# Running sums of softplus values as products of split fp32r halves, with the next head's scores issued earlier, in a two-layer hybrid encoder on one Trainium2 core

## The chip, the cores and the metric

The kernel runs on one core of a Trainium2 chip. Its time is the device time of one execution in microseconds. Three runs of the kernel before took 3045.1, 3046.19 and 3046.79 us; the median, 3046.19 us, is the number to compare with.

The engines are named as in the profile: PE is TensorE's matmul side and PEld its weight loads, DVE is VectorE, ACT is ScalarE, POOL is GpSimd, SP is SyncE, whose queue issues the weight transfers.

## The reference

The input is 512 tokens of 1024 features. Each of two layers runs a half-step SwiGLU FFN, a mixer, a second half-step FFN and a gated embedding. The mixer projects its input and runs three token mixers beside each other: RWKV-7, stick-breaking attention and HGRN2. The change is in the attention, with four heads of 128 features. For query q and key k let z = q·k / sqrt(128). In the reference:

```
m      = where(k < q, -softplus(z), 0)
within = sum of m over the keys of the same block of 128 from k onwards
carry  = sum of m over all later blocks of keys
att    = where(k < q, exp(z + within + carry), 0)
y      = att @ v
```

So the logit of a key is its score, less the softplus values of this key and of all later keys up to the query. That running sum along the keys is what the change computes in another way.

## The kernel before

**Dense products.** All large products run in fp32r. An fp32 value is split into a high fp32r part and the rest, and a product is three fp32r products (high by high, rest by high, high by rest), issued in `products` (L864 to L885, the matmul is L881). The weights arrive in slots of 256 rows by 512 columns through a ring of three raw buffers: SP's queue loads them (L1254), POOL splits each slot in four instructions (L1226 high part, L1229 rest, for two halves) into a ring of three split buffers. POOL waits for a split buffer until PE has used the slot that was in it three slots ago (L1217), and SP waits for POOL (L1250).

**Filling.** `dense` (L893) is a generator: each step issues one block, three fp32r products of 512 columns. PE's program runs small, latency-bound work of the mixers and calls `advance(fill, n)` (L990) to put n blocks of dense work between its parts. During the attention the filling is `hg_projections` (L1054): four groups of projections, n = 0 to 3, each with four result tiles and 32 blocks, in PSUM banks 0 to 3. Blocks 29 to 32 of a group complete its four tiles.

**Attention, per head h, on PE** (L1086 to L1108). PSUM banks 4 to 7 are for it (`core_banks`).

- Scores: for each block of 128 keys kb = 3, 2, 1, 0, one fp32 product of the queries from kb on (128, 256, 384, 512 columns) into a bank of its own (L1090).
- 16 blocks of filling.
- Sums: for kb = 3 to 0 it waits for the softplus values of block kb (`sb_sp`, L1094). Then, for each k2 from kb to 3, it adds one fp32 product onto the scores: constants (a triangle of -1 for k2 = kb, all -1 for k2 > kb) times the softplus values of block k2 (L1096). These are 10 products in a head, with 2560 columns together. In the trace each fp32 product is two records.
- 8 blocks of filling, the product of `att` with the values (L1103), 8 blocks of filling.

**On ACT** (L1568 to L1609), in this order for a head: absolute values of the scores (L1574), exp (L1578), ln(1 + ...) (L1582), each for the four kb; in head 2 a logarithm for the HGRN2 gate (L1449), in head 3 the absolute values, two exponentials and a logarithm for it; the exponential of the logits (L1595), which waits for the sums; the copy of y out of PSUM (L1603); `hgrn_inputs(L, h)` (L1398 to L1415, L1607), which waits for the four tiles of filling group n = h, one after the other, and evacuates them; after head 1, an absolute value and an exponential of 2048 columns (L1442, L1443). Then come the absolute values of head h + 1.

**On DVE** (L1924 to L1946): for kb = 3 to 0 the softplus value max(z, 0) + ln(...) with z read from PSUM (L1932) and the causal mask on its diagonal block (L1935), whose end is the signal `sb_sp` for PE. From head 1 on, a wait for the last sums of the previous head stands before it (L1931). Later the mask on the exponentials (L1943), whose end is the signal `sb_att`. In head 2 the operations of `forget_gate` follow (L1874), in head 3 those of `forget_rate` (L1885) stand before L1943.

Of the kernel before, what the change touches and what calls it, by code (L numbers as in the profile page):

```python
# [21 lines left out]
F32 = mybir.dt.float32  # L22
# [6 lines left out]
P = 128  # L29
D = 1024  # L30
SEQ = 512
# [106 lines left out]
def build(nc, a, out, counts, banks_of):  # L138
# [4 lines left out]
    with ctx:  # L143
# [57 lines left out]
        with ExitStack() as own:  # L201
            y_raw = sb(own, "y_raw", [P, 3, 4, SEQ])
            sb_sp, sb_att = y_raw[:, 1, :, :], y_raw[:, 2, :, :]
            o3 = ExitStack()
            rw_u = sb(o3, "rw_u", [P, 3, SEQ + 1])
            rw_d = sb(o3, "rw_d", [P, SEQ])
            lora_x = sb(o3, "lora_x", [P, 3, SEQ])
            with ExitStack() as o1:
                hg_q = sb(o1, "hg_q", [P, 4, SEQ])
                hg_k = sb(o1, "hg_k", [P, 4, SEQ])  # L210
                hg_p = sb(o1, "hg_p", [P, 4, SEQ])
                hg_x = sb(o1, "hg_x", [P, 4, SEQ])
                hg_v = sb(o1, "hg_v", [P, NT, 512])
                hg_g = sb(o1, "hg_g", [P, NT, 512])
                hg_e = sb(o1, "hg_e", [P, 2, 1024])
                with ExitStack() as o2:
                    sb_q = sb(o2, "sb_q", [P, 4, SEQ])
                    sb_k = sb(o2, "sb_k", [P, 4, SEQ])
                    sb_v = sb(o2, "sb_v", [P, NT, 512])
                    sb_e = sb(o2, "sb_e", [P, 4, SEQ])  # L220
                with ExitStack() as o2:
                    hg_Q = sb(o2, "hg_Q", [P, 4, SEQ])
                    hg_K = sb(o2, "hg_K", [P, 4, SEQ])
                    hg_att = sb(o2, "hg_att", [P, 2, NT, 4, HALF])
                    hg_S = sb(o2, "hg_S", [P, NT, 4, P])
            with ExitStack() as o2:


                rkv = sb(o2, "rkv", [P, 3, SEQ])
                starts = sb(o2, "starts", [P, SEQ])  # L230
                w_up = sb(o2, "w_up", [P, 512])
                g_up = sb(o2, "g_up", [P, 2, 512])
                rk_sum = sb(o2, "rk_sum", [P, 4, P])
                rw_sw = sb(o2, "rw_sw", [P, SEQ])
                rw_a = sb(o2, "rw_a", [P, SEQ])
                rw_cs = sb(o2, "rw_cs", [P, SEQ])
                rw_e3 = sb(o2, "rw_e3", [P, SEQ])
                rw_e1 = sb(o2, "rw_e1", [P, SEQ])
                rw_kk = sb(o2, "rw_kk", [P, SEQ])
                rw_ss = sb(o2, "rw_ss", [P, SEQ])  # L240
                bonus_v = [sb(o2, "bonus_v0", [P, SEQ])]
                rw_keep = sb(o2, "rw_keep", [P, SEQ])
                pq_add = sb(o2, "pq_add", [P, 2, NT, 2, HEAD])
                xl = sb(o2, "xl", [P, 2 * NT, HEAD])
                inv = sb(o2, "inv", [P, 2 * NT, HEAD])
                invT = sb(o2, "invT", [P, 2 * NT, HEAD])
                pq = sb(o2, "pq", [P, 2, NT, 2, HEAD])
                bm = sb(o2, "bm", [P, 2, NT, 2, HEAD])
                km = sb(o2, "km", [P, 2, NT, 2, HEAD])
                rw_dec = sb(o2, "rw_dec", [P, 2, SEQ])  # L250
                ar = sb(o2, "ar", [P, NT, 2, P])
                b_inv = sb(o2, "b_inv", [P, SEQ])
                k_inv = sb(o2, "k_inv", [P, SEQ])
                b_tok = sb(o2, "b_tok", [P, NT, P])
                k_tok = sb(o2, "k_tok", [P, NT, P])
                yt = sb(o2, "yt", [P, 2, NT, P])
                bonus_v.append(sb(o2, "bonus_v1", [P, SEQ]))
                rhs = sb(o2, "rhs", [P, 2, NT, P])
                xx = sb(o2, "xx", [P, 2, NT, P])
                v_tok = sb(o2, "v_tok", [P, 2, NT, P])  # L260
                gn_st = sb(o2, "gn_st", [P, 2, NT, 2])

            rw_bd, rw_kd = rw_dec[:, 0, :], rw_dec[:, 1, :]
            rw_b, rw_k2 = rw_ss, rw_sw
            d_mat = rhs[:, 0, :, :].rearrange("p t (c n) -> p (t c) n", c=2)
            s_all = rhs[:, 1, :, :].rearrange("p t (c n) -> p (t c) n", c=2)
            o3.close()
            with ExitStack() as o2:
                yT = [sb(o2, "yT_hi", [P, 4, SEQ], F32R), sb(o2, "yT_lo", [P, 4, SEQ], F32R)]
                gate_s = sb(o2, "gate_s", [P, 4, SEQ])  # L270
                m_tmp = sb(o2, "m_tmp", [P, SEQ])
                m_acc = sb(o2, "m_acc", [P, KD, SEQ])
                mT = [sb(o2, "mT_hi", [P, KD, SEQ], F32R), sb(o2, "mT_lo", [P, KD, SEQ], F32R)]
# [43 lines left out]
        def of_units(x, height, which):  # L317

            return x.rearrange("p u (n two s) -> p u n two s", two=2, s=height)[:, :, :, which, :]

        def of_parity(x, odd):

# [508 lines left out]
        def _(pe):  # L831
# [213 lines left out]
            for L in range(DEPTH):  # L1045
# [37 lines left out]
                for m in range(4):  # L1083
                    for n in range(3):
                        pe.wait_ge(*after("sb_in", L, n, m))
                for h in range(4):  # L1086
                    zb = {}
                    for kb in range(3, -1, -1):
                        zb[kb] = take(("sbz", L, h, kb), ("sb_exp", L, h, kb), core_banks)
                        nc.tensor.matmul(zb[kb][:, kb * P:SEQ], sb_k[:, h, kb * P:(kb + 1) * P], sb_q[:, h, kb * P:SEQ],  # L1090
                                         start=True, stop=False, skip_group_check=True).then_inc(*step("sbz_done", L, h, kb))
                    advance(fill, 16)
                    for kb in range(3, -1, -1):
                        pe.wait_ge(*after("sb_sp", L, h, kb))  # L1094
                        for k2 in range(kb, 4):
                            ins = nc.tensor.matmul(zb[kb][:, k2 * P:SEQ], cons[:, K_NTRI if k2 == kb else K_NONE, :],  # L1096
                                                   sb_sp[:, k2, k2 * P:SEQ], start=False, stop=k2 == 3, skip_group_check=True)
                        ins.then_inc(*step("sb_logit", L, h, kb))
                    advance(fill, 8)
                    o = take(("sby", L, h), ("sb_y", L, h), core_banks)  # L1100
                    for kb in range(4):
                        pe.wait_ge(*after("sb_att", L, h, kb))
                        ins = nc.tensor.matmul(o[:, kb * P:SEQ], sb_v[:, kb, h * P:(h + 1) * P], sb_att[:, kb, kb * P:SEQ],  # L1103
                                               start=kb == 0, stop=kb == 3, skip_group_check=True)
                    ins.then_inc(*step("sby_done", L, h))
                    if h == 3:
                        hgrn_pairs(-1)
                    advance(fill, 8)  # L1108
                run(fill)

                def all_projections():
# [628 lines left out]
        def _(dve):  # L1740
# [160 lines left out]
            for L in range(DEPTH):  # L1901
# [12 lines left out]
                else:  # L1914
# [5 lines left out]
                    chain(v.tensor_tensor(lb_log, lb_s, lb_rest, ALU.subtract))  # L1920
                    v.tensor_scalar(lb_rest, lb_rest, -1.0, None, ALU.mult).then_inc(*step("lb_set", L))
                now("lb_set", L)

                for h in range(4):  # L1924
                    for kb in range(3, -1, -1):
                        b = ps[banks_of.get(("sbz", L, h, kb), 0)]
                        cols = slice(kb * P, SEQ)
                        diag = slice(kb * P, kb * P + P)
                        now("sb_ln", L, h, kb)
                        if h:  # L1930
                            now("sb_logit", L, h - 1, 0)  # L1931
                        v.scalar_tensor_tensor(sb_sp[:, kb, cols], b[:, cols], 0.0, sb_e[:, kb, cols], ALU.max, ALU.add).then_inc(  # L1932
                            *step("sb_sp0", L, h, kb))
                        now("sb_sp0", L, h, kb)
                        v.tensor_tensor(sb_sp[:, kb, diag], sb_sp[:, kb, diag], cons[:, K_CAUSAL, :], ALU.mult).then_inc(  # L1935
                            *step("sb_sp", L, h, kb))
                    if h == 3:
                        forget_rate(L)
                    for kb in range(3, -1, -1):
                        diag = slice(kb * P, kb * P + P)  # L1940
                        now("sb_exp", L, h, kb)

                        v.scalar_tensor_tensor(sb_att[:, kb, diag], sb_att[:, kb, diag], 3e38, cons[:, K_CAUSAL, :], ALU.min,  # L1943
                                               ALU.mult).then_inc(*step("sb_att", L, h, kb))
                    if h == 2:
                        forget_gate(L)  # L1946
# [185 lines left out]
```

## Time and profile before

| | us |
|---|---|
| median of three runs | 3046.19 |
| the profiled execution, its own time | 3044.86 |
| span of the profiled execution | 3043.1 |
| PE busy | 2947.1 |
| POOL busy | 2312.5 |
| DVE busy | 1362.2 |
| ACT busy | 652.6 |

The profile is that of one execution. Busy times overlap, so they don't add up to the span. Matmuls are pipelined: a record of 0.39 us is followed by the next 0.23 us later, so the spacing of the starts is what a matmul costs. Layer 0's attention lies at 451 to 569 us of the span, layer 1's at about 1963 to 2081.

### The profile page before, as it was taken

How to read it: one execution, taken by the hardware profiler on the slowest of the kernel's cores; microseconds unless marked ns; L12 is line 12 of the kernel's file. 1: busy time of each engine (PE TensorE's matmuls, PEld its weight loads, DVE VectorE, ACT ScalarE, POOL GpSimd, SP SyncE). 2: the span in 40 equal slices, each digit the busy share in tenths (PEclk: the TensorE clock that was granted, in tenths of full speed). 3: DMA queues.
4: the chain of work that ended last, by engine and by line, in shares of the span. 5: the costliest groups of instructions: out<-in, count | busy, mean ns of one | idle time of the engine just before them, and what ended most of it. 6: DMA issues, size and time to landing. Idle time of an engine off the chain costs nothing.

```text
span 3043.1 us, 48203 instructions
## 1 busy us (share of the span) xinstructions
PE 2947.1 (97%) x20354; PEld 2392.3 (79%) x20354; DVE 1362.2 (45%) x1833; ACT 652.6 (21%) x1069; POOL 2312.5 (76%) x1853
## 2 busy tenths in 40 slices
PE   8999999999899999999999999999998999999997
PEld 7888877776678888888788888777766788888886
DVE  4221133786647462220752212437766465622118
ACT  1000125554310020000420002246543100200003
POOL 8998896662259989888689887966521699899874
PEclk9999999999999999999999999999999999999999
DMA  4332242121113333333323332421210233333332
GB/s 137 104 97 98 90 132 71 48 59 38 30 57 97 125 97 104 98 96 97 104 88 100 100 96 89 133 69 48 56 42 23 70 94 128 97 104 97 97 97 97
DMA packets 202068, 266.65 MB, mean 88 GB/s; under 512 B 12369, under 2 KB 130493, under 8 KB 201853
## 3 DMA queue, kind: packets, MB, share of 16 engines
q1 hardware_dynamic: 194624, 243.51, 26.5%
q10 hardware_dynamic: 7228, 20.05, 1.8%
q8 instruction: 162, 2.65, 0.4%
q14 instruction: 54, 0.43, 0.0%
HBM read 257.22 MB, written 6.29 MB: 87 GB/s over the span
## 4 chain that ended last, share of the span: by engine, by line
PE 83%; DVE 7%; POOL 5%; issue 2%; ACT 2%; DMA 0%; SPq 0%; DVEq 0%; POOLq 0%; ACTq 0%
PE ps L881 73%; POOL w_hi L1226 3%; POOL w_lo L1229 3%; PE ps L449 1%; PE ps L1096 1%; PE ps L1074 1%; PE ps L928 1%; PE ps L1090 1%; PE ps L1103 1%; PE ps L433 0%; PE ps L1142 0%; PE ps L443 0%; DVE hT_lo L1762 0%; PE ps L574 0%; DVE bm L690 0%
## 5 line engine op out<-in xcount | busy, mean ns | idle before, releaser
L1226 POOL TENSOR_TENSOR w_hi<-w_raw,zero 128x512 fp32r<-128x512 f32 (+2 forms) x912 | 1048.3, 1149 | 618.6 <-PE ps L881 573.5
L1229 POOL TENSOR_TENSOR w_lo<-w_raw,w_hi 128x512 fp32r<-128x512 f32 (+2 forms) x936 | 1290.0, 1379 | 83.2 <-ACT w_hi L1370 11.6
L881 PE MATMUL ps<-hT_hi,w_hi 128*128 128x512 f32 (+1 forms) x2368 | 928.0, 392 | 14.4 <-POOL w_lo L1229 11.7
L881 PE MATMUL ps<-hT_hi,w_lo 128*128 128x512 f32 (+1 forms) x2368 | 906.0, 383 | 0.0
L881 PE MATMUL ps<-hT_lo,w_hi 128*128 128x512 f32 (+1 forms) x2368 | 905.9, 383 | 0.0
L881 PEld LDWEIGHTS ps<-hT_hi,w_hi 128*128 128x128 f32 x2368 | 444.0, 188 | 126.1 <-POOL w_lo L1229 22.4
L881 PEld LDWEIGHTS ps<-hT_hi,w_lo 128*128 128x128 f32 x2368 | 444.0, 187 | 88.5
L881 PEld LDWEIGHTS ps<-hT_lo,w_hi 128*128 128x128 f32 x2368 | 444.5, 188 | 84.6 <-issue 2.9
L1839 DVE TENSOR_TENSOR act_raw<-silu,ps 128x512 f32<-128x512 f32 x88 | 59.9, 681 | 620.6 <-PE ps L881 620.6
L881 PE MATMUL ps<-w_hi,aT_hi 128*128 128x512 f32 x704 | 274.6, 390 | 0.0
L881 PE MATMUL ps<-w_lo,aT_hi 128*128 128x512 f32 x704 | 274.0, 389 | 0.0
L881 PE MATMUL ps<-w_hi,aT_lo 128*128 128x512 f32 x704 | 273.9, 389 | 0.0
L1387 ACT ACTIVATE silu<-ps 128x512 f32<-128x512 f32 x88 | 52.6, 598 | 883.1 <-PE ps L881 879.5
L1859 DVE SCALAR_TENSOR_TENSOR h_tok<-ps,h_tok 128x512 f32<-128x512 f32 x48 | 32.8, 683 | 437.4 <-PE ps L881 437.4
L881 PEld LDWEIGHTS ps<-w_lo,aT_hi 128*128 128x128 f32 x704 | 132.1, 188 | 27.5
L881 PEld LDWEIGHTS ps<-w_hi,aT_lo 128*128 128x128 f32 x704 | 132.2, 188 | 27.3
L881 PEld LDWEIGHTS ps<-w_hi,aT_hi 128*128 128x128 f32 x704 | 132.2, 188 | 27.2
L1843 DVE TENSOR_TENSOR aT_lo<-act_raw,aT_hi 128x512 fp32r<-128x512 f32 x88 | 129.1, 1467 | 3.0
L881 PE MATMUL ps<-w_hi,hT_hi 128*128 128x512 f32 x320 | 127.8, 399 | 1.1 <-DVE hT_lo L1762 1.1
L881 PE MATMUL ps<-w_lo,hT_hi 128*128 128x512 f32 x320 | 124.7, 390 | 0.0
L881 PE MATMUL ps<-w_hi,hT_lo 128*128 128x512 f32 x320 | 124.6, 389 | 0.0
L1326 ACT ACTIVATE ln_rstd<-ln_mv,ln_eps 128x1 f32<-128x1 f32 x32 | 9.5, 296 | 445.0 <-DVE ln_mv L1797 432.2
(314 smaller groups left out, 3443.9 us busy)
## 6 DMA issues: line engine op xcount, KB each, us to landing
w_raw<-in_w_in SPq DMA_DIRECT2D x104, 512.0 KB, 3.6
w_raw<-in_ffn_wg SPq DMA_DIRECT2D x176, 256.0 KB, 2.8
w_raw<-in_ffn_wu SPq DMA_DIRECT2D x176, 256.0 KB, 3.1
w_raw<-in_ffn_wd SPq DMA_DIRECT2D x88, 512.0 KB, 3.6
w_raw<-in_w_in SPq DMA_DIRECT2D x96, 128.0 KB, 2.3
w_raw<-in_w_out SPq DMA_DIRECT2D x16, 512.0 KB, 3.6
w_raw<-in_ple_gate SPq DMA_DIRECT2D x16, 512.0 KB, 3.6
ln_rows<-in_ln_g ACTq DMA_DIRECT2D x8, 512.0 KB, 4.1
```

The lines of the kernel that those rows point to most:

```text
L449: ins = nc.tensor.matmul(b[unit(cp), HEAD * u:HEAD * u + HEAD], xl[unit(cp), u, :], invT[unit(cp), u, :], start=True, stop=True)
L881: ins = nc.tensor.matmul(o, l_, r_, start=first, stop=last, skip_group_check=into is not None)
L928: ins = nc.tensor.transpose(b[:, c:c + P], h_tok[:, t, k * P:(k + 1) * P], ident())
L1074: ins = nc.tensor.matmul(b[unit(cp), c:c + HALF], kk_[:, h, early], qq_[:, h, early], start=True, stop=True)
L1090: nc.tensor.matmul(zb[kb][:, kb * P:SEQ], sb_k[:, h, kb * P:(kb + 1) * P], sb_q[:, h, kb * P:SEQ], start=True, stop=False, skip_group_chec ...
L1096: ins = nc.tensor.matmul(zb[kb][:, k2 * P:SEQ], cons[:, K_NTRI if k2 == kb else K_NONE, :], sb_sp[:, k2, k2 * P:SEQ], start=False, stop=k2 ...
L1226: nc.gpsimd.tensor_tensor(w_split[0][:, q, kk, 0:w], w_raw[:, r, kk, 0:w], zero[:, 0:1].to_broadcast([P, w]), ALU.add).then_inc(*step("w_h ...
L1229: nc.gpsimd.tensor_tensor(w_split[1][:, q, kk, 0:w], w_raw[:, r, kk, 0:w], w_split[0][:, q, kk, 0:w].bitcast(F32), ALU.subtract).then_inc( ...
L1387: nc.scalar.activation(silu[:, m, :], b[:, :], ACT.Silu).then_inc(*step("silu_done", L, f, g, m))
L1839: v.tensor_tensor(act_raw[:, m, :], silu[:, m, :], b[:, :], ALU.mult).then_inc(*step("act_raw", L, f, g, m))
L1843: v.tensor_tensor(aT[1][:, k, :], act_raw[:, m, :], aT[0][:, k, :].bitcast(F32), ALU.subtract).then_inc(*step("act_rest", L, f, k))
L1859: v.scalar_tensor_tensor(z, b[:, :], 0.5 if name == "down" else 1.0, z, ALU.mult, ALU.add).then_inc(*step("res_sum", L, q, half, m))
```

## The change

- Each softplus block, masked as before, is now also copied into an fp32r tile `sp_hi` (rounded) and subtracted from it into `sp_lo` (the rest). The signal `sb_sp` now comes from that subtraction. The two tiles hold the four blocks behind each other in 1280 columns; they are written only after the previous head's last sums, and the wait for these stands before the copy now instead of before the softplus operation.
- The -1 constants are copied once per layer into an fp32r tile `sp_ones`.
- Each of the 10 fp32 products of the sums becomes two fp32r products, one with each half: 20 products of 5120 columns together.
- The scores of head h + 1 are issued at the end of head h. The blocks of filling are 17 (head 0) or 24 (later heads) between the scores and the sums, 4 between the sums and the product with the values and 4 behind it (in head 3: 8 and 7). All four heads together still have 128 blocks. The filling in front of the sums of head 1, 2, 3 starts behind block 25, 57, 89.

```diff
@@ -201,6 +201,9 @@
             sb_sp, sb_att = y_raw[:, 1, :, :], y_raw[:, 2, :, :]
+            with ExitStack() as o2:
+                sp_part = [sb(o2, "sp_hi", [P, 1280], F32R), sb(o2, "sp_lo", [P, 1280], F32R)]
+                sp_ones = sb(o2, "sp_ones", [P, 2, P], F32R)
             o3 = ExitStack()
@@ -317,6 +320,11 @@
+        def sp_cols(kb):
+
+            at = P * (0, 4, 7, 9)[kb]
+            return slice(at, at + SEQ - kb * P)
@@ -1083,20 +1091,25 @@
-                for h in range(4):
-                    zb = {}
+                zb = {}
+
+                def scores(h):
                     for kb in range(3, -1, -1):
                         zb[kb] = take(("sbz", L, h, kb), ("sb_exp", L, h, kb), core_banks)
                         nc.tensor.matmul(zb[kb][:, kb * P:SEQ], sb_k[:, h, kb * P:(kb + 1) * P], sb_q[:, h, kb * P:SEQ],
                                          start=True, stop=False, skip_group_check=True).then_inc(*step("sbz_done", L, h, kb))
-                    advance(fill, 16)
+
+                scores(0)
+                for h in range(4):
+                    advance(fill, 24 if h else 17)
                     for kb in range(3, -1, -1):
                         pe.wait_ge(*after("sb_sp", L, h, kb))
                         for k2 in range(kb, 4):
-                            ins = nc.tensor.matmul(zb[kb][:, k2 * P:SEQ], cons[:, K_NTRI if k2 == kb else K_NONE, :],
-                                                   sb_sp[:, k2, k2 * P:SEQ], start=False, stop=k2 == 3, skip_group_check=True)
+                            for part in range(2):
+                                ins = nc.tensor.matmul(zb[kb][:, k2 * P:SEQ], sp_ones[:, int(k2 > kb), :], sp_part[part][:, sp_cols(k2)],
+                                                       start=False, stop=k2 == 3 and part == 1, skip_group_check=True)
                         ins.then_inc(*step("sb_logit", L, h, kb))
-                    advance(fill, 8)
+                    advance(fill, 4 if h < 3 else 8)
                     o = take(("sby", L, h), ("sb_y", L, h), core_banks)
@@ -1105,7 +1118,9 @@
                     if h == 3:
                         hgrn_pairs(-1)
-                    advance(fill, 8)
+                    advance(fill, 4 if h < 3 else 7)
+                    if h < 3:
+                        scores(h + 1)
                 run(fill)
@@ -1920,6 +1935,7 @@
                 now("lb_set", L)
+                v.tensor_copy(sp_ones[:, :, :], cons[:, K_NTRI:K_NTRI + 2, :])
@@ -1927,13 +1943,15 @@
                         now("sb_ln", L, h, kb)
-                        if h:
-                            now("sb_logit", L, h - 1, 0)
                         v.scalar_tensor_tensor(sb_sp[:, kb, cols], b[:, cols], 0.0, sb_e[:, kb, cols], ALU.max, ALU.add).then_inc(
                             *step("sb_sp0", L, h, kb))
                         now("sb_sp0", L, h, kb)
-                        v.tensor_tensor(sb_sp[:, kb, diag], sb_sp[:, kb, diag], cons[:, K_CAUSAL, :], ALU.mult).then_inc(
-                            *step("sb_sp", L, h, kb))
+                        chain(v.tensor_tensor(sb_sp[:, kb, diag], sb_sp[:, kb, diag], cons[:, K_CAUSAL, :], ALU.mult))
+                        if h:
+                            now("sb_logit", L, h - 1, 0)
+                        chain(v.tensor_copy(sp_part[0][:, sp_cols(kb)], sb_sp[:, kb, cols]))
+                        v.tensor_tensor(sp_part[1][:, sp_cols(kb)], sb_sp[:, kb, cols], sp_part[0][:, sp_cols(kb)].bitcast(F32),
+                                        ALU.subtract).then_inc(*step("sb_sp", L, h, kb))
```

`chain` signals a semaphore at the end of an instruction and has the same engine wait for it.

## Rows read from the trace of the kernel before

**Rows 1.** The page: busy us (share of the span) and instructions; chain that ended last.
```profile
PE 2947.1 (97%) x20354; PEld 2392.3 (79%) x20354; DVE 1362.2 (45%) x1833; ACT 652.6 (21%) x1069; POOL 2312.5 (76%) x1853
...
PE 83%; DVE 7%; POOL 5%; issue 2%; ACT 2%; DMA 0%; SPq 0%; DVEq 0%; POOLq 0%; ACTq 0%
```

**Rows 2.** Busy time by stretch, layer 0's attention, sum of 450 to 570 us.
```profile
sum 120.00, PE 118.71 PEld 92.60 DVE 46.63 ACT 69.02 POOL 75.62; mean PE 29.68 PEld 23.15 DVE 11.66 ACT 17.25 POOL 18.90
```

**Rows 3.** Timeline of PE, heads 1 and 2: start us, us, operation [idle before].
```profile
481.79 2.32 PE L1090 MATMUL ps<-sb_q,sb_k 128*128 128x128 f32 x8
...
484.19 0.40 PE L881 MATMUL ps<-hT_lo,w_hi 128*128 128x512 f32 x1
...
494.85 4.50 PE L1096 MATMUL ps<-y_raw,cons 128*128 128x128 f32 x20
...
499.42 0.40 PE L881 MATMUL ps<-hT_lo,w_hi 128*128 128x512 f32 x1
...
525.37 4.50 PE L1096 MATMUL ps<-y_raw,cons 128*128 128x128 f32 x20
```

**Rows 4.** Timeline of ACT, from the end of heads 0 and 1 on.
```profile
481.99 0.60 ACT L1406 ACTIVATE hg_q<-ps 128x512 f32<-128x512 f32 x1
...
484.15 0.60 ACT L1574 ACTIVATE sb_e<-ps 128x512 f32<-128x512 f32 x1 [0.37 <-PE ps L1090]
...
513.14 1.91 ACT L1442 ACTIVATE hg_e<-hg_k 128x2048 f32<-128x2048 f32 x1
...
517.04 1.43 ACT L1574 ACTIVATE sb_e<-ps 128x128 f32<-128x128 f32 x4
```

**Rows 5.** DVE: the mask product's ns min/median/max, then the timeline, heads 1 to 3.
```profile
L1935 DVE TENSOR_TENSOR y_raw<-y_raw,cons x32: 291/546/1001, 459.1 to 2063.8; 128x128 f32<-128x128 f32 x32
...
489.27 0.29 DVE L1932 SCALAR_TENSOR_TENSOR y_raw<-ps,sb_e 128x128 f32<-128x128 f32 x1 [19.48 <-ACT sb_e L1582]
...
490.26 0.68 DVE L1935 TENSOR_TENSOR y_raw<-y_raw,cons 128x128 f32<-128x128 f32 x1
...
492.94 0.41 DVE L1935 TENSOR_TENSOR y_raw<-y_raw,cons 128x128 f32<-128x128 f32 x1
...
500.02 0.29 DVE L1943 SCALAR_TENSOR_TENSOR y_raw<-y_raw,cons 128x128 f32<-128x128 f32 x1 [1.28 <-ACT y_raw L1595]
...
521.54 0.29 DVE L1932 SCALAR_TENSOR_TENSOR y_raw<-ps,sb_e 128x128 f32<-128x128 f32 x1 [21.23 <-ACT sb_e L1582]
...
548.88 0.29 DVE L1932 SCALAR_TENSOR_TENSOR y_raw<-ps,sb_e 128x128 f32<-128x128 f32 x1 [6.07 <-ACT sb_e L1582]
```

**Rows 6.** Timeline of POOL, head 1.
```profile
489.72 1.07 POOL L1226 TENSOR_TENSOR w_hi<-w_raw,zero 128x512 fp32r<-128x512 f32 x1 [2.85 <-PE ps L881]
490.87 1.29 POOL L1229 TENSOR_TENSOR w_lo<-w_raw,w_hi 128x512 fp32r<-128x512 f32 x1
...
495.16 1.04 POOL L1226 TENSOR_TENSOR w_hi<-w_raw,zero 128x512 fp32r<-128x512 f32 x1 [0.59 <-PE ps L881]
```

**Rows 7.** Timeline of PE: transposes of 128 columns, fp32r products of 256.
```profile
374.99 1.91 PE L928 MATMUL ps<-cons,h_tok 128*128 128x128 f32 x16
...
378.68 0.28 PE L881 MATMUL ps<-hT_hi,w_hi 128*128 128x256 f32 x1
...
379.15 0.28 PE L881 MATMUL ps<-hT_lo,w_hi 128*128 128x256 f32 x1
```

**Rows 8.** DVE's cast and subtraction in the merge stage: ns min/median/max.
```profile
L2051 DVE CAST yT_hi<-y_raw x48: 419/1332/1514, 866.0 to 2536.7; 128x512 fp32r<-128x512 f32 x48
...
L2052 DVE TENSOR_TENSOR yT_lo<-y_raw,yT_hi x48: 691/1412/1667, 866.5 to 2538.2; 128x512 fp32r<-128x512 f32 x48
```

**Rows 9.** Timeline of PE, head 3 of layer 0.
```profile
566.29 2.39 PE L1103 MATMUL ps<-y_raw,sb_v 128*128 128x512 f32 x8 [0.41 <-DVE y_raw L1943]
```

**Rows 10.** PE after its longest wait for ACT: timeline, and busy time by stretch (PEclk).
```profile
1519.96 3.65 PE L928 MATMUL ps<-cons,h_tok 128*128 128x128 f32 x16 [4.34 <-ACT h_tok L1330]
...
1518.00:1522.00 4.00, 2.04 (x10) 2.08 (x11) 2.85 (x8) 2.51 (x5) 0.00 (x0) 0.50 0.12 41
```

## The prediction

> **What bounds the kernel now.** I read the page first: the busy shares and the chain that ended last [rows 1]. TensorE is busy for 97% of the span, and 83% of the chain is PE. Then the attention stage by stretch [rows 2]: of 120 us PE is busy 118.7, at a granted clock of 1.00. So here whatever PE no longer has to do is time won, and whatever PE has to wait for is time lost, one to one. Then PE's own timeline over head 1 [rows 3], with L for the moment at which PE reaches the first running-sum product of a head. Scores run from 481.79 to 483.96 (2.17 us: the second fill record, 484.19, less one pitch), 16 filling blocks to L = 494.85 (10.9 us, 0.681 each), the sums until 499.19 (4.34 us, 499.42 less one pitch). Last, the helpers in front of L: ACT [rows 4], DVE [rows 5], POOL [rows 6]. DVE has the last softplus ready at 493.35, 1.5 us before L. That margin is what the change spends.
>
> **Part 1: the sums as fp32r products.** Removed: 10 fp32 products a head, 2560 columns, 4.34 us. Added: 20 fp32r products, 5120 columns. fp32r records of 256 columns follow each other every 0.1175 us [rows 7] (378.68 to 379.15, four steps), those of 512 every 0.227 (a block is three); 384 lies between, 0.172. None has 128 columns. By the line through the other two it would be 0.064; the fp32 transposes of 128 columns take 1.91 us for 16, thus 0.11 each [rows 7]; an fp32 product of 128 columns is 0.21 (4.34 us over 2560 columns). I take 0.107, near the transposes, because each product also needs a full set of weights. Sum: 2 x 0.227 + 4 x 0.172 + 6 x 0.1175 + 8 x 0.107 = 2.7 us (ends 2.4 and 3.5). PE gains 1.6 us a head (0.8 to 1.9), 13 us over eight heads, if it need not wait.
>
> **Part 2: the copy and the subtraction on DVE.** Per block row (128, 256, 384, 512 columns) DVE gets a cast and a subtraction in front of the signal for PE. At their shortest they take 0.42 and 0.69 us at 512 columns [rows 8]; for fewer I take casts of 0.22, 0.29, 0.36 and subtractions of 0.29, 0.42, 0.56 (estimates: about 0.15 fixed, and the slope of the old operations, half of it for the cast). That is 3.2 us, 3.4 with the waits between chained operations.
> But DVE isn't alone. The same 128-column mask product takes between 0.29 and 1.00 us; the one at 490.26 takes 0.68 and ends at 490.94, 0.15 us after the POOL instruction 489.72 to 490.79 [rows 5, 6]. The operations with PSUM as one source keep their time. In the merge stage, beside a busy POOL, the same cast and subtraction have medians of 1.33 and 1.41 us [rows 8]. I read: a DVE operation with two SBUF sources, or a cast from SBUF to SBUF, that finds POOL at work waits until POOL's instruction ends and then needs its own time less 0.14; POOL's next one waits in turn. By this rule the second and the last mask product of head 1 end at 490.95 and 493.30; the trace has 490.94 and 493.35 [rows 5].
> The Trainium skill, SBUF — State Buffer, "Who interferes with whom", says the same: such an instruction and a GpSimd instruction that reads SBUF exclude each other for their whole length. It speaks against this change, and the trace agrees.
> The old chain had four such operations a head, the new one has twelve. POOL's rhythm is one slot of four (about 0.91 and 1.14 us each, held) per eight blocks, starting 0.3 us after PE passes the slot's end.
>
> **Part 3: scores moved forward.** They stand 24 blocks before L instead of 16, so 5.4 us earlier. But ACT's order is unchanged: before the absolute values of the next head it evacuates the group of 32 filling blocks. That group used to be complete when the scores were issued; now 25 blocks precede them, so it is complete 7 blocks later. ACT starts 0.1 us behind the last evacuation (481.99 + 0.60) [rows 4], thus 2.17 + 4.8 + 0.8 = 7.7 us behind the scores. The absolute values then take 1.43 us in one piece, as in head 2 [rows 4]. From their end to DVE's first operation it is 4.5 us in head 1 (484.75 to 489.27), 3.1 in heads 2 and 3 [rows 4, 5]; in head 2 another 3.9 for the forget gate's exponentials come first (513.14 to 517.04). With L at 2.17 + 16.3 = 18.5 us behind the scores, DVE starts 5.0, 2.5 and 6.4 us before L in heads 1, 2, 3 (old: 5.6, 3.8 and 7.0, as L is 30.5 us later from head to head [rows 3]); in head 0, with 17 blocks instead of 16, 6.3. So the move buys DVE nothing. The PE work moved costs nothing: the same matmuls.
> Now the chain, with POOL slots from about L-5.7 and L-0.3. Head 1, ends of softplus, mask, cast, subtraction relative to L: -4.7, -3.4, -2.4, -1.1 (three POOL instructions met); -0.8, -0.5, -0.1 (POOL between its slots), +1.1; +1.5, +2.3, +3.5, +5.0 (three met); +5.6, +5.9, +6.4, +7.1 (POOL has run out of freed slots, since PE stands still). Signals to PE thus at L-1.1, +1.1, +5.0, +7.1; head 0: -3.4, -0.5, +3.5, +5.9; head 2: -0.6, +3.3, +5.6, +7.7; head 3: -4.5, -0.7, +3.5, +6.0. About eight of twelve contested operations meet a POOL instruction. After the last signal PE has eight products left, 1.25 us. Sums end at L+7.2, 8.4, 9.0, 7.3 against L+4.34: **+2.9, +4.1, +4.6, +2.9 us**, 14.5 us per layer.
>
> **Small parts, at nothing.** The weights' copy falls in DVE's idle time before head 0. The wait on the previous head's sums moves, but they are long done. Values times sums now follow 4 blocks behind the sums (2.7 us): the last mask product ended 1.1 us behind them (500.31) [rows 5]; if that cover were gone, up to 2 us a head. POOL is held up by eight more operations, 2 us a head, and stands still longer than that waiting for PE (75.6 us busy of 120) [rows 2]; uncovered 17 us. SP's weight requests follow POOL. The new buffers lie where the RWKV inputs come later, and add no wait. In head 3 PE waited 0.41 us for the masked exponentials [rows 9]; with the sums later that goes, -0.8 in all.
>
> **The sum,** on all eight heads: 2 x 14.5 - 0.8 = +28 us on the profiled execution's 3044.9 us (span 3043.1; the median of the three runs is 3046.2, 0.04% more): **3073 us**. With 0.064 or 0.213 for the small products it is 3072 or 3075: most of them are hidden in DVE's delay.
>
> **Rivals.**
> Not slower, the cast and subtraction keep out of POOL's way (place: the twelve contested operations; it decides where they wait less than about 0.25 us each): the chain ends at L+0.3, +1.6, +4.0, +0.2, the heads change by -1.6, -1.5, +1.0, -1.6, in all 2 x -3.7 - 0.8 = -8: 3037 us. For it: in head 3 all four mask products ran clean, as POOL stood still then. Against it: the medians in [rows 8]. Chance 0.16.
> Half the waits: fewer POOL instructions meet the chain than my phases say. Heads change by the mean of the two cases, +0.7, +1.3, +2.8, +0.7, in all +10: 3055 us; at its lower end no change. Chance 0.16.
> The clock falls: PE sat idle 4.34 us before L928 at 1519.96, the clock stood at half, and 16 transposes took 3.65 us instead of 1.91 [rows 7, 10]; until full speed returned some 2.2 us were lost. My waits are up to 3.4 us in one piece. If each head but the first brings one fall, +13: 3086 us. Chance 0.08.
> My forecast: 0.60.
>
> **Numbers.** A measurement of this kernel tells about 0.2% (6 us) from no change. Slower by more than that: forecast, clock and most of the half case, 0.78; same: 0.06; faster 0.16. The forecast's own range is 3061 to 3084; down to 3045 and up to 3086 the range takes in the half case and the clock.
>
> **What would show it.** Right: PE idle before the sum products, released by DVE's subtraction, 3 to 6 us a head; casts and subtractions of 1 us and more where POOL works; ACT's absolute values starting 7 blocks behind the scores. Part 1 is wrong if 20 products with all signals there take over 3.5 us. The forecast is wrong if the subtractions stand at 0.3 to 0.7 us and PE doesn't wait.

## The result and the profile after

The changed kernel took 3085.93 us (median of 4 runs, 3083.42 to 3088.2) against 3046.49 us for the kernel before on the same chip: ratio 1.0133, 95% interval 1.0121 to 1.0144. It is slower by 39.4 us. The forecast was 3073 us, 28 us slower; its own range was 3061 to 3084, and with two rivals taken in it went from 3045 to 3086. The profiled execution took 3083.42 us with a span of 3081.6 us (before: 3044.86 and 3043.1), so the two traces differ by 38.5 us, and that is the sum to account for.

The waits of PE in the trace of after (us in total, times, longest). Before, PE never waited for the softplus values; in a layer's attention it waited only 0.9 us before the first scores and the 0.41 us of [rows 9].

```profile
PE ps L1109 <- DVE sp_lo L1953: 32.0, 20, 3.1
```

The chain that ended last, on the page of after, as shares of the span by engine (before [rows 1]: 83% PE):

```profile
PE 80%; DVE 9%; POOL 5%; ACT 3%; issue 2%; DMA 0%; SPq 0%; DVEq 0%; POOLq 0%; ACTq 0%
```

PE's timeline in head 1 (start, duration, line, operation, tiles, what it stood idle for), which answers to [rows 3]:

```profile
499.95 0.22 PE L1109 MATMUL ps<-sp_hi,sp_ones 128*128 128x128 f32 x1
...
502.36 0.39 PE L1109 MATMUL ps<-sp_hi,sp_ones 128*128 128x256 f32 x1 [2.08 <-DVE sp_lo L1953]
...
505.41 0.69 PE L1109 MATMUL ps<-sp_hi,sp_ones 128*128 128x384 f32 x1 [2.37 <-DVE sp_lo L1953]
...
507.52 0.80 PE L1109 MATMUL ps<-sp_hi,sp_ones 128*128 128x512 f32 x1 [0.36 <-DVE sp_lo L1953]
...
509.72 0.41 PE L1109 MATMUL ps<-sp_lo,sp_ones 128*128 128x128 f32 x1
509.93 0.73 PE L889 MATMUL ps<-hT_hi,w_hi 128*128 128x512 f32 x1
```

From the second on, each block row of sums waits for its own signal, and the sums end 9.98 us behind L = 499.95 instead of 4.34. The 512-column filling record behind them has 0.73 us instead of 0.39. That is the clock, as the windows over the same stretch show (length of the stretch, PE busy us, instructions, granted clock, DMA share, GB/s):

```profile
504.00:506.00 2.00, 0.59 (x2) 0.74 0.28 27
506.00:508.00 2.00, 1.64 (x7) 0.50 0.67 236
508.00:510.00 2.00, 2.00 (x9) 0.50 0.00 0
510.00:512.00 2.00, 2.00 (x7) 0.56 0.00 0
512.00:514.00 2.00, 2.00 (x9) 1.00 0.00 0
```

The granted clock falls from its upper level (2.4 GHz) to its lower (1.2 GHz) inside the second wait and is back near 511. It also falls in heads 0 and 2, and not in head 3. In head 0 it is down already within the first wait, before any second one:

```profile
468.42 0.69 PE L1109 MATMUL ps<-sp_hi,sp_ones 128*128 128x384 f32 x1 [2.79 <-DVE sp_lo L1953]
```

The windows with the busy us of PE, PEld, DVE, ACT and POOL before the clock:

```profile
466.00:468.00 2.00, 0.00 (x0) 0.00 (x0) 1.97 (x2) 0.05 (x1) 1.95 (x2) 0.85 0.42 163
468.00:470.00 2.00, 1.58 (x6) 1.56 (x6) 1.93 (x4) 0.00 (x0) 1.48 (x1) 0.50 0.00 0
```

In head 2 it stands at 1.00 through a wait of 3.05 us and the four products behind it (1.00 from 541 to 542), and is down behind the next wait, of 1.59 us (0.50 from 543 to 544):

```profile
540.41 0.39 PE L1109 MATMUL ps<-sp_hi,sp_ones 128*128 128x256 f32 x1 [3.05 <-DVE sp_lo L1953]
...
542.67 0.69 PE L1109 MATMUL ps<-sp_hi,sp_ones 128*128 128x384 f32 x1 [1.59 <-DVE sp_lo L1953]
```

DVE in head 1, against [rows 5], and POOL beside it, against [rows 6]:

```profile
495.03 0.29 DVE L1946 SCALAR_TENSOR_TENSOR y_raw<-ps,sb_e 128x128 f32<-128x128 f32 x1 [20.57 <-ACT sb_e L1597]
495.36 1.35 DVE L1949 TENSOR_TENSOR y_raw<-y_raw,cons 128x128 f32<-128x128 f32 x1
496.74 0.95 DVE L1952 CAST sp_hi<-y_raw 128x128 fp32r<-128x128 f32 x1
497.72 1.41 DVE L1953 TENSOR_TENSOR sp_lo<-y_raw,sp_hi 128x128 fp32r<-128x128 f32 x1
...
506.77 0.69 DVE L1953 TENSOR_TENSOR sp_lo<-y_raw,sp_hi 128x512 fp32r<-128x512 f32 x1
```

```profile
495.26 1.30 POOL L1244 TENSOR_TENSOR w_lo<-w_raw,w_hi 128x512 fp32r<-128x512 f32 x1
...
497.69 1.29 POOL L1244 TENSOR_TENSOR w_lo<-w_raw,w_hi 128x512 fp32r<-128x512 f32 x1
```

DVE starts 4.9 us ahead of L. A mask product and a subtraction of 128 columns, whose shortest is 0.29 us each, take 1.35 and 1.41 us, each ending 0.15 us behind a POOL instruction. The last subtraction, beside an idle POOL, takes 0.69 us for four times the columns. The chain lasts 12.4 us.

The whole account for layer 0, from PE's timelines of the two kernels, as us behind L:

| | head 0 | head 1 | head 2 | head 3 |
|---|---|---|---|---|
| sums end, forecast | 7.2 | 8.4 | 9.0 | 7.3 |
| sums end, after | 8.5 | 10.0 | 10.2 | 5.8 |
| the 4 blocks behind the sums over 2.72 us | +0.5 | +1.0 | +1.1 | (8 blocks) |

Against 4.34 each before, the sums cost 17.1 us a layer (34.5 less 17.4) where I had 14.5. The filling behind them costs 2.6, which I did not have, and head 3's 0.41 us is gone. That is 19.2 us a layer, 38.5 in all, as much as the traces differ by. Layer 1 has the same sums to 0.02 us.

### The profile page after: what moved, and what is told of

Its sections match the earlier page's. It is cut to its first block, busy times and chain, and to the rows that moved or that the text cites. A ratio compares the mean times of both kernels' runs of the same rounds, so it can differ in the third digit from the quotient of the medians.

```text
span 3081.6 us, 48267 instructions
## 1 busy us (share of the span) xinstructions
PE 2954.9 (96%) x20354; PEld 2404.3 (78%) x20354; DVE 1408.3 (46%) x1899; ACT 651.5 (21%) x1069; POOL 2311.5 (75%) x1853
## 4 chain that ended last, share of the span: by engine, by line
PE 80%; DVE 9%; POOL 5%; ACT 3%; issue 2%; DMA 0%; SPq 0%; DVEq 0%; POOLq 0%; ACTq 0%
PE ps L889 70%; POOL w_hi L1241 3%; POOL w_lo L1244 3%; PE ps L457 1%; DVE sp_hi L1952 1%; DVE sp_lo L1953 1%; PE ps L1082 1%; DVE y_raw L1949 1%; PE ps L1109 1%; PE ps L936 1%; PE ps L1099 1%; PE ps L1116 1%; PE ps L441 0%; PE ps L1157 0%; DVE y_raw L1946 0%
## 5 line engine op out<-in xcount | busy, mean ns | idle before, releaser
L889 PE MATMUL ps<-hT_hi,w_hi 128*128 128x512 f32 (+1 forms) x2368 | 930.1, 393 | 14.5 <-POOL w_lo L1244 11.9
```

Of the source, the lines that this page charges most:

```text
L889: ins = nc.tensor.matmul(o, l_, r_, start=first, stop=last, skip_group_check=into is not None)
```

## The experiments

**Each part alone.** First before with only the scores moved, then after with the old places of scores and filling. Edits:

```
First, on before (PE's program; "..." marks lines left out):
-                for h in range(4):
-                    zb = {}
+                zb = {}
+
+                def scores(h):
...
-                    advance(fill, 16)
+
+                scores(0)
+                for h in range(4):
+                    advance(fill, 24 if h else 17)
...
-                    advance(fill, 8)
+                    advance(fill, 4 if h < 3 else 8)
...
-                    advance(fill, 8)
+                    advance(fill, 4 if h < 3 else 7)
+                    if h < 3:
+                        scores(h + 1)
```

The second, on after, has the same lines the other way round.

> The kernel before with the moved scores and the new places of the filling alone; the sums stay fp32 products of the masked softplus tile, no cast, no subtraction. If the loss comes from the longer chain on DVE (my theory), this is within 3 us of the kernel before (about 3046): DVE starts 0.5 to 1.3 us later against L, but with 4 contested operations it is done before PE's fp32 products need the last block. If moving the scores behind ACT's evacuations is itself the loss (rival), it takes a large part of the 39 us: over 3060.

> The changed kernel with the scores and the filling back in their old places (16, 8, 8): only the fp32r products and their cast and subtraction. Theory: the same waits on DVE, as the lead is 5.5 to 7 us here against 2.5 to 6.4: 3078 to 3086, a few us under the changed kernel. Rival, that the new places of the scores make the loss: near or under 3046.

The first took 3051.2 us, ratio 1.0019 (1.001 to 1.0029); the second 3088.26 us, ratio 1.0147 (1.0131 to 1.0163). So the fp32r part makes the whole loss. The move alone costs 5 us, and with fp32r sums it takes back 2 us, which the two intervals do not tell from nothing: part 3 of the prediction ("buys DVE nothing") holds. Both runs lie 2 us above what I expected. In the first, 3.5 of the 5.4 us over before are a longer wait: values of head 3 wait 2.1 us a layer for the masked exponentials (0.4 before). The cover is not what went, since 8 blocks stand between sums and values of head 3 in both kernels. The masks on the exponentials come later against L: they start at L+10.0 instead of L+9.4 and take 1.98 instead of 0.90 us for the four.

```profile
PE ps L1107 <- DVE y_raw L1949: 4.3, 2, 2.1
...
566.64 1.98 DVE L1949 SCALAR_TENSOR_TENSOR y_raw<-y_raw,cons 128x128 f32<-128x128 f32 x4
```

**POOL stands still while DVE works on the sums' inputs.** To after was added, in front of the last of a filling group's weight slots:

```
+                if g[0][0] == "hg" and i == 3:
+                    pool.wait_ge(*after("sb_sp", g[0][1], g[0][2], 0))
```

> The changed kernel, and POOL waits with the fourth slot of each of the four filling groups until DVE's last subtraction of that head, so that POOL does no work beside DVE's chain. If the shared access of POOL and DVE makes the chain long (theory), casts and subtractions fall to 0.2 to 0.7 us, the last signal comes about 0.3, 1.6, 4.0 and 0.2 us behind L, PE waits under 3 us a head and the clock mostly holds: about 3037, under the kernel before. If the operations are as long by themselves, or ACT's lateness is the cause (rival), it stays over 3070.

It took 3057.56 us, ratio 1.0043 (1.0028 to 1.0058): 28 us won on after, short of the 3037 expected. DVE in head 1, first and last block row:

```profile
489.63 0.29 DVE L1951 TENSOR_TENSOR y_raw<-y_raw,cons 128x128 f32<-128x128 f32 x1
...
490.22 0.29 DVE L1955 TENSOR_TENSOR sp_lo<-y_raw,sp_hi 128x128 fp32r<-128x128 f32 x1
...
494.70 0.43 DVE L1954 CAST sp_hi<-y_raw 128x512 fp32r<-128x512 f32 x1
495.16 0.69 DVE L1955 TENSOR_TENSOR sp_lo<-y_raw,sp_hi 128x512 fp32r<-128x512 f32 x1
```

Nothing of DVE's program was changed, and its chain falls from 12.4 to 6.5 us: the contention is the cause of the late signals. What was missing to 3037 is in the main two things. In head 2 the sums still end 6.2 us behind L, where two waits of 1.1 us are followed by a fall of the clock (0.58 from 528 to 530):

```profile
527.74 0.50 PE L1109 MATMUL ps<-sp_hi,sp_ones 128*128 128x512 f32 x1 [1.08 <-DVE sp_lo L1955]
```

And there is a new wait. POOL, behind with its slots, works without a pause beside the forget gate's operations on DVE:

```profile
533.72 1.38 DVE L1897 TENSOR_SCALAR hg_p<-hg_p,lbT 128x512 f32<-128x512 f32 x1
...
536.20 1.77 DVE L1900 TENSOR_TENSOR hg_k<-hg_p,hg_k 128x512 f32<-128x512 f32 x1
```

The two and the one between them take 0.49, 0.49 and 0.69 us in the 24/4/4 kernel further down, which has no pause. ACT's forget steps and head 3's exponentials are then late, and PE waits 11.0 us for them, in two waits:

```profile
PE ps L1116 <- DVE y_raw L1963: 11.0, 2, 5.5
```

**The waits filled, the clock kept.** On after, products with a third, all-zero set of weights were put in front of the waits (24 of them before the second row of sums in heads 1 and 2, 12 before the third row in every head). They add nothing to the result and shorten no wait for DVE:

```
+                        idle = (24 if h in (1, 2) and kb == 3 else 12 if kb == 2 else 0)
+                        for n in range(idle):
+                            ins = nc.tensor.matmul(zb[kb][:, kb * P:SEQ], sp_ones[:, 2, :], hT[0][:, 0, kb * P:SEQ], start=False,
+                                                   stop=n == idle - 1, skip_group_check=True)
...
+                v.tensor_copy(sp_ones[:, 2, :], zero[:, 0:1].to_broadcast([P, P]))
```

> The changed kernel with products by a zero weight tile put into PE's waits: 24 of 128 columns behind the sums of kb = 3 in heads 1 and 2, 12 of 256 columns behind those of kb = 2 in every head, added to the same bank (they add zero); DVE's chain stays as it is. If the falling clock costs about 12 us of the 39 (theory: my forecast of the waits was right and the clock is the missing term), PEclk stays at 1.00 through the attention and the time is 3072 to 3077. If the clock costs nothing (rival: the waits alone are the loss), it stays at 3084 to 3088.

It took 3077.41 us, ratio 1.0109 (1.0093 to 1.0125), 8.5 us under after and at the upper end of what I expected; the profiled executions differ by 9.9 (3073.55), the ratios to before by 7 us. The windows over the sums of heads 0 to 2 stand at full clock, with PE's last wait in head 1 still there:

```profile
464.00:474.00 10.00, 7.20 (x45) 1.00 0.38 105
498.00:508.00 10.00, 8.38 (x62) 1.00 0.37 107
534.00:544.00 10.00, 8.38 (x62) 1.00 0.36 104
```

```profile
506.33 0.50 PE L1109 MATMUL ps<-sp_hi,sp_ones 128*128 128x512 f32 x1 [1.09 <-DVE sp_lo L1958]
```

The sums now end 7.4, 8.9, 9.1 and 5.8 us behind L (forecast 7.2, 8.4, 9.0, 7.3), and the profiled execution is 28.7 us slower than that of before (3073.55 less 3044.86), where the forecast had 28 (the medians, 3077.41 and 3045.77, lie 31.6 apart). So the forecast describes the profiled execution of this kernel, and the clock is the other 7 to 10 us of after. Two of the four executions, 3079 and 3082 us, show a mean clock of 0.994 instead of 0.997, so the filled waits do not hold it every time.

**An idle PE by itself.** The kernel before, with six memsets that nothing reads, ahead of the last mask product of heads 1 and 2:

```
+                rest = sb(o2, "rest", [P, 1280])
...
+                        if kb == 0 and h in (1, 2):
+                            for n in range(6):
+                                chain(v.memset(rest[:, :], 0.0))
```

> The kernel before (fp32 sums, old order) with six 1280-column memsets on DVE (nothing reads them) ahead of the last mask product of heads 1 and 2 in both layers: some 6.7 us of work that holds back PE's last signal of these heads, of which some 3.6 us are covered. So PE stands idle in one piece for some 3 us, four times, with nothing else changed: some 12 us of idle time. Theory (an idle piece of this length takes the clock to half speed for some us behind it): the time rises by more than the idle time itself, by 18 to 26 us, and windows behind the idle pieces show a granted clock of 0.5 to 0.9. Rival (an idle piece costs what it lasts; the lower clock of after came from something else, such as the fp32r products): 12 us, clock 1.00 throughout.

It took 3081.55 us, ratio 1.012 (1.0105 to 1.0135), +35.9 us. The waits were twice what I had planned, since the chained memsets follow each other in 1.46 us instead of 1.1:

```profile
PE ps L1098 <- DVE y_raw L1940: 24.2, 4, 7.3
```

The windows behind the wait of head 1:

```profile
500.00:502.00 2.00, 0.34 (x1) 0.93 0.65 169
502.00:504.00 2.00, 2.00 (x3) 0.50 0.24 93
504.00:506.00 2.00, 2.00 (x8) 0.72 0.00 0
506.00:508.00 2.00, 2.00 (x11) 1.00 0.00 0
```

Four idle pieces of 24.2 us together cost 35.9 us: 12 more than they last. From one head's L to the next, heads 1 and 2 take 6.8 and 9.8 us more than before in layer 0 and 8.0 and 10.4 in layer 1, with pieces of 4.8 and 7.3 us in each layer. So the low clock costs 2.0, 2.5, 3.2 and 3.2 us, 10.9 in all. No fp32r product and no cast was added in this kernel, so a low clock needs neither. The pieces here are longer than any in after; for those of after the filled waits are the evidence.

**The scores in step with the evacuation.** Part 3 of the prediction said why the move did not help DVE: the group of 32 blocks is complete 7 blocks behind the scores. With 24/4/4 blocks in every head it is complete just when the scores are issued. Edit, on after:

```
-                    advance(fill, 24 if h else 17)
+                    advance(fill, (24, 24, 24, 24)[h])
...
-                    advance(fill, 4 if h < 3 else 8)
+                    advance(fill, 4)
...
-                    advance(fill, 4 if h < 3 else 7)
+                    advance(fill, 4)
```

> The kernel after with the filling cut 24/4/4 in every head (after: 17/4/4, 24/4/4, 24/4/4, 24/8/7), so that the group of 32 filling blocks is complete just when the next head's scores are issued and ACT can start on them at once instead of 7 blocks later. Nothing of the sums, the cast or the subtraction is changed. Theory (the loss is DVE's late signals, and the clock falls because PE idles for them): DVE's chain starts some 7 us earlier (leads over L of 11, 8.5 and 12.4 us in heads 1 to 3, 11.1 in head 0), a contended chain of some 12 us then ends its last signal near L+1, which PE needs at L+1.1; only head 2 still waits, some 2 us a layer. The fp32r gain (about 1.9 us a head) comes through and the clock holds: 3030 to 3042, say 3036; waits of PE for sp_lo under 6 us in all (after: 32.0). In head 3 the values now come 4 blocks behind the sums, so up to 2 us a layer may be waited for the masked exponentials. Rival (the loss lies in the fp32r products themselves or in what DVE's added work does to other stages): the time stays within 8 us of after, 3078 to 3094.

> The kernel before (fp32 sums, no cast, no subtraction) with scores moved and the filling cut 24/4/4 in every head: the control of the aligned kernel, which differs from it by the fp32r sums alone. The alignment alone should give nothing, since PE did not wait for the signals before: 3046 to 3052 (a wait of up to 2 us a layer for the masked exponentials in head 3, as with the scores moved alone). If the aligned kernel with fp32r sums is then 8 to 16 us below this one, the products themselves gain what their pitch says (20 products 2.4 us instead of 4.34, eight times, 15.5 us at most).

With fp32r sums 3045.42 us, ratio 1.0 (0.9991 to 1.001); with fp32 sums 3045.0 us, ratio 0.9999 (0.999 to 1.0009). DVE now starts 11.0 us ahead of L in head 1 instead of 4.9. That takes back all 40 us of after, but the fp32r sums win nothing on their control. The control lies 1 us under its range, with no wait for the masked exponentials. The waits are down from 32.0 us, and most of what is left sits in head 2 (2.9 us a layer):

```profile
PE ps L1109 <- DVE sp_lo L1953: 7.8, 6, 2.9
```

There the sums take 6.0 us (529.02 to 535.05) and the four blocks behind them 4.4 (535.05 to 539.44) instead of 2.72: again one fall of the clock. In layer 1 the same wait brings the clock down sooner, and the sums take 7.1 us. My 3036 was too low, since I had left out that fall and the 0.7 us by which the sums of heads 0 and 1 are still late.

**The same with POOL standing still.**

> The aligned kernel with, on top, the wait that lets GpSimd stand still until the head's last subtraction in every group of filling slots. Theory: DVE's chain runs uncontended (6.5 us in a head instead of some 12), so PE waits for sp_lo for under 2 us in all; what is then gained over the aligned kernel is at most its remaining waits. Against it stands what the same pause cost where it was tried before, GpSimd catching up beside the forget steps before head 3. Since DVE's chain now starts and ends 5 us or more before the sums, the pause is shorter: 3026 to 3045, say 3034. Rival (the pause itself is what costs, wherever it stands): within 3 us of the unaligned kernel with the pause, 3057.

3051.57 us, ratio 1.0019 (1.0009 to 1.0029), above its range. No wait for sp_lo is left, and the pause again makes one of 7 us in head 3 of each layer:

```profile
PE ps L1116 <- DVE y_raw L1963: 14.0, 2, 7.0
```

**More lead, or a shorter chain.** Two remedies for head 2. One cuts the filling 28/2/2 in heads 0 to 2 and 24/8/0 in head 3. The other keeps 24/4/4, lets ACT make the cast in heads 0 to 2, and has DVE subtract one block row behind:

```
ACT, behind the logarithms ("..." marks DVE's part, left out):
+                    if h < 3:
+                        for kb in range(3, -1, -1):
+                            now("sb_msk", L, h, kb)
+                            nc.scalar.activation(sp_part[0][:, sp_cols(kb)], sb_sp[:, kb, kb * P:SEQ], ACT.Copy).then_inc(
+                                *step("sb_hi", L, h, kb))
...
```

> The kernel after with the filling cut 28/2/2 in heads 0 to 2 and 24/8/0 in head 3 (aligned as 24/4/4 was: 32 blocks a head). PE reaches the sums 2.7 us later after the scores in heads 0 to 2, so DVE's signals, whose chain is as contended as before, come in time in heads 0 and 1, and head 2 (whose sums took 6.0 us in the 24/4/4 kernel, with the clock falling behind them) waits 1 us or less. Theory: the sums come down to some 2.4 to 2.8 us a head (24/4/4: 3.4, 3.4, 6.0, 2.7), the clock stays at full speed, and some 6 us a layer is won on the 24/4/4 kernel's 3045.4: 3030 to 3040, say 3033. PE's waits for sp_lo under 2.5 us in all (24/4/4: 7.8). Rival (what is won in the sums is lost in the values, which now come only 2 blocks, 1.4 us, behind them, waiting for the exponentials and the masked ones): 3043 to 3049 and waits of PE for y_raw of some 1 us a head.

> The 24/4/4 kernel with the cast taken off DVE in heads 0 to 2: ACT makes sp_hi from the masked softplus values, DVE only subtracts, one block row behind. Eight instead of twelve contested DVE operations a head. Theory (the late signals are made of DVE's waits for GpSimd): DVE's last signal comes some 3 us earlier in heads 0 to 2, PE's waits for sp_lo fall from 7.8 us to under 3, head 2's sums from 6.0 to some 3 us and the clock stays: 3032 to 3040, say 3036. Rival (hand-overs between DVE and ACT cost as much as the cast's waits did): 3044 to 3050, with the same waits.

3034.17 us, ratio 0.996 (0.9948 to 0.9973), and 3033.04 us, ratio 0.9959 (0.9944 to 0.9974). Both beat the kernel before. In the first the waits for sp_lo come to:

```profile
PE ps L1109 <- DVE sp_lo L1953: 0.9, 2, 0.4
```

In the second no wait for the sums is left. Of the 20 products, the last row of eight in PE's timeline of head 1:

```profile
500.22 0.45 PE L1109 MATMUL ps<-sp_hi,sp_ones 128*128 128x512 f32 x1
500.50 0.39 PE L1109 MATMUL ps<-sp_lo,sp_ones 128*128 128x512 f32 x1
...
501.33 0.22 PE L1109 MATMUL ps<-sp_hi,sp_ones 128*128 128x128 f32 x1
501.39 0.27 PE L1109 MATMUL ps<-sp_lo,sp_ones 128*128 128x128 f32 x1
501.50 0.45 PE L889 MATMUL ps<-hT_hi,w_hi 128*128 128x512 f32 x1
```

From 498.78 to 501.50 the 20 products take 2.72 us. DVE's part of the chain there is 7.6 us (487.76 to 495.35), and ACT's four casts take 0.29 to 0.63 us while POOL works beside them. All 24 casts of the kernel lie between 0.29 and 0.64 us, so none is held up:

```profile
488.88 0.29 ACT L1602 ACTIVATE sp_hi<-y_raw 128x128 fp32r<-128x128 f32 x1
493.46 0.63 ACT L1602 ACTIVATE sp_hi<-y_raw 128x512 fp32r<-128x512 f32 x1 [1.97 <-DVE y_raw L1961]
```

The Trainium skill, SBUF — State Buffer, "Who interferes with whom", says that ACT never waits for another engine's access; this trace agrees.

**Both remedies, and the cast on ACT alone.**

> Both remedies together: the filling cut 28/2/2, 28/2/2, 28/2/2, 24/8/0 and the cast on ACT in heads 0 to 2. In the 28/2/2 kernel only head 2's sums (3.4 us) stood above the 2.7 us that 20 products take without a wait, so about 0.7 us a layer is left to win: 3031 to 3035, say 3033. If it were below 3030, something other than the sums would still be in the way in both remedies.

> The kernel after, with its own cut of the filling (17/4/4, 24/4/4, 24/4/4, 24/8/7), and only the cast moved from DVE to ACT in heads 0 to 2. With the cast on ACT, DVE's chain in head 1 took 7.6 us (487.76 to 495.35 in the 24/4/4 kernel) instead of 12.4 (after: 495.03 to 507.46). Theory (the loss of after is the length of the contended chain against its lead over L): from the leads of 6.3, 5.0 and 2.5 us the sums end near L+2.9, L+3.9 and L+6.5 in heads 0 to 2, and as in after (L+5.8) in head 3: about +2 us a layer against before, and one fall of the clock a layer at most: 3046 to 3058, say 3051, a gain of some 35 us on after. Rival (the place of the scores, not the chain's length, is what costs): above 3070.

Both together: 3031.92 us, ratio 0.9955 (0.9943 to 0.9968), the lowest median here, though its interval overlaps those of the other two. The cast on ACT in after's own order: 3057.79 us, ratio 1.0039 (1.0026 to 1.0052), 28 us under after, at the upper end of its range. In its trace the sums of heads 0 to 3 end 2.7, 4.4, 9.1 and 5.8 us behind L (I expected 2.9, 3.9, 6.5 and 5.8), and only behind head 2, where the clock stands at 0.50 from 530 to 536, do the four blocks take long (4.0 us). Head 2 is the one I had too short, as in the 24/4/4 kernel. PE's waits are halved against after:

```profile
PE ps L1109 <- DVE sp_lo L1948: 15.5, 14, 2.1
```

## Why the prediction was wrong

- **Part 1, the products: right.** "Sum: ... 2.7 us" stands against 2.72 measured where nothing waits. The 128-column product alone was taken as 0.107: a first half follows in 0.06 us and a second in 0.11, so the pair costs 0.17, but the larger products cost a little more than their pitch (0.28 and 0.23 for the 512-column pair). The two errors cancel, so that the sum meets is in part luck.
- **Part 2, DVE's chain against POOL: right in its rule, near in its times.** The waits, the released engine and the length of the chain came as said: signals to PE in head 1 at L-0.8, +2.4, +5.4, +7.5 against -1.1, +1.1, +5.0, +7.1. The pause of POOL shows the cause. Only head 3 came out short (5.8 against 7.3): POOL's last slot there has instructions of 0.67 to 1.00 us on 288 columns, and six of the twelve operations were held up.
- **Part 3, the moved scores: right.** DVE's lead in head 1 was 4.9 us (I had 5.0), and undoing the move changes 2 us.
- **The step that failed is the last rival, "The clock falls", and its chance of 0.08.** The sum has no term for the clock. The forecast had left it at full speed because the only row of before with a fall had 4.34 us of idle time in one piece [rows 10] and my waits were at most 3.4. The largest in after is 3.1, and still the clock fell in three heads of four. In head 0 a single piece of 2.79 us was enough; in head 1 it was two, of 2.08 and 2.37 us with four small products between them. The row I took as the only case was no lower bound, and shorter pieces in one stretch have to be read together. The filled waits give its size: 10 us of the 38.5 (7 by the ratios). My price for it in the rival, +13 for six falls, was near (2.2 us each there, 1.7 here: 9.9 us over six). That its time of 3086 is the one measured is partly luck: it let head 0 off and counted head 3, and it was the other way round.
- **The rivals "keep out of POOL's way" (3037) and "half the waits" (3055): wrong.** In heads 0 to 2 the waits came at full size, as above, and casts have a median of 0.95 us in after with 0.23 as their shortest.
- **Small parts.** Head 3's 0.41 us went, as said. The values behind 4 blocks cost nothing in heads 0 to 2, in after or in the kernel with the scores moved alone. What the latter waits in head 3, 2.1 us a layer behind 8 blocks, was not among the parts.

What stays open: how much idle time, in what pieces, brings the clock down here. The length of the pieces does not decide it alone. One piece of 2.79 us was enough in head 0 of after, one of 2.53 in head 3 of the kernel with the old places, and two of 1.1 in head 2 of the kernel with the pause; but head 2 of after kept its clock through 3.05 us, and head 3 of after through 1.59 and 1.09. No run varied this alone.

```profile
579.47 0.80 PE L1105 MATMUL ps<-sp_hi,sp_ones 128*128 128x512 f32 x1 [2.53 <-DVE sp_lo L1947]
```

## What to carry to other kernels

When a small product is made cheaper by work on another engine, compare the length of that engine's chain, contended, with its lead over the consumer first: here 12.4 us against 5, and 6 us more lead were worth 40 us. A scheduling move helps only if it moves what the helper really waits for, here the evacuation that stands ahead of the scores in ACT's order. And price idle time on TensorE by more than its length as soon as a wait of 2.5 us, or several shorter ones in a stretch, may arise; here that added a third (after) to nearly a half (the memsets).

## What the runs showed of the hardware

- A DVE `tensor_scalar` with one SBUF source and one result in SBUF is held up by POOL like the two-source operations: 1.15 to 1.51 us instead of 0.48 at 512 columns (head 2 of the kernel with the pause against the 24/4/4 kernel).
- fp32r products of 128 columns, each with weights of its own, follow each other in 0.06 and 0.11 us in turn at full clock.
- A pause given to POOL is not free where nothing waits for POOL directly. In layer 0 its catching up lengthened 12 operations of the forget gate (9 with 24/4/4) by some 0.9 us each, and in both kernels PE then has one wait a layer, of 5.5 and 7 us.
